# Expert 0's rows by products with a 0/1 mask instead of a gathered load, in a mixture of experts behind two transformer-like blocks

## The chip, the cores and the metric

The kernel runs on one core of one Trainium2 chip. It is a single launch that computes a network of about four layers for 512 tokens. The metric is the time of the whole launch on the device, in microseconds. The engines named here are TensorE (PE in the profile, PEld for its weight loads), VectorE (DVE), ScalarE (ACT), GpSimd (POOL) and SyncE (SP), which issues most DMA transfers. Each engine runs its own queue in order and waits on semaphores.

## The reference, cut to what matters

The change lies in the last layer, a mixture of 64 experts in 8 groups. Each of the 512 tokens picks a group, then two experts in it; an expert is a gated feed-forward net of width 512.

```python
def hier_moe(h, w_rg, w_re, w_gate, w_up, w_down):
    ...
    g_sel = jnp.argmax(g_logits, axis=-1)
    ...
    p_top, e_top = lax.top_k(jax.nn.softmax(e_logits, axis=-1), TOP_K)
    gate = p_group * p_top / jnp.sum(p_top, axis=-1, keepdims=True)
    expert_id = (g_sel[:, None] * EXPERTS_PER_GROUP + e_top).reshape(-1).astype(jnp.int32)
    ...
    xb = hf[tok_buf].reshape(n_blocks, MOE_BLOCK, D)

    def expert_block(args):
        xe, e = args
        return (jax.nn.silu(xe @ w_gate[e]) * (xe @ w_up[e])) @ w_down[e]

    yb = lax.map(expert_block, (xb, block_eid)).reshape(n_slots, D)
    y = jnp.zeros_like(hf).at[tok_buf].add(yb * gate_buf[:, None].astype(yb.dtype))
```

Everything is in float32. Before this layer stand a gated delta net, a retention layer, two convolutional feed-forward nets and a mixer of long convolutions and gated scans; the change leaves them alone.

## The kernel before, in words

The normalized tokens are kept as rows, `m.hn`, [128, 4, 1024]: token 128 t + p is on partition p. The same rows are written to `x_rows` in HBM. `Router.vector` finds for each token its group and its first and second expert, as 0/1 tables `wide[0]` and `wide[1]` over 64 experts, and their sum `wide[2]`. `Router.tensor` counts these: L4022 sums each expert's tokens, L4024 and L4026 give each token its order among those of an expert, in PSUM bank 0. VectorE makes slot numbers of it: every expert has 64 slots (`SLOTS`), slot 64 e + i holds the i-th token of expert e, and what exceeds 64 goes to overflow blocks behind the main loop. Eight products (L4031) of one 0/1 table of places and one table of blocks each turn "token to slot" into "slot to token", and VectorE writes the list as whole numbers: `x_of` (L4133) and `y_of` (L4134).

`Experts` runs the 64 experts in order. For expert e, GpSimd gathers 64 rows of `x_rows` by column e of `x_of` into `m.xe[e % 2]` (`gather_x`, L4155). TensorE turns them (`turn_x`, L4270, eight transposes into PSUM bank 0), VectorE copies them to `m.xeT` (`copy_x`, L4407), TensorE multiplies by the up and gate weights (`project`, L4282 and L4283, eight steps of two products with 512 columns), ScalarE and VectorE make the activation (L4392, L4420), TensorE turns it and multiplies by the down weights (L4293, L4299), ScalarE copies the result out (L4382) and GpSimd scatters it to `y_rows` (L4160). The order on TensorE is software pipelined by hand: `step` of expert e computes its projection, and ahead of the last of the eight steps (`ahead`) waits for the activation of expert e-1 and for the gathered rows of expert e+1 (`x_landed`).

SyncE loads the weights, 2.1 MB for each of the three matrices of an expert. Up and gate weights have two buffers, and expert 2 (`THIRD`) has a third pair of its own: `w_gate` in the tile hT and `w_up` in `m.hn`, which therefore must not be read any more. `load_up_apart` issues these two (L4218 after the transposes of the router, L4221 after the gathers of the first two experts have landed); all later loads stand behind them in SyncE's queue, each released by the projection or down product that frees its buffer (L4209).

`unread_products` (L310) are 128x128 products whose result nobody reads; 16 stand ahead of L4031 and 20 ahead of expert 0. The last two experts' outputs are combined in another way (`LATE`); their gate tables `m.late_gate` (L4439) and `m.late_diag` (L4426) are made by VectorE ahead of expert 0 and are first needed by `pause` behind expert 15.

Of the kernel before, what the change touches and what calls it, by code (L numbers as in the profile page):

```python
# [35 lines left out]
P = 128  # L36
# [44 lines left out]
LATE = 2  # L81
# [275 lines left out]
class Stream:  # L357
# [128 lines left out]
    def each(self, eng, chunks, per, body, splits=False):  # L486

        self.per = per
        for c in range(chunks):
            body(self.n + c, 0, c)  # L490
        self.skip(chunks, per, splits)
# [3491 lines left out]
class Router:  # L3983
# [3 lines left out]
    def __init__(self, k, m, norm):  # L3987
        self.k, self.m, self.norm = k, m, norm
        room = m.late
        self.logits = room.take(TT, N_GROUPS + NE)  # L3990
        self.small = room.take(8, TT, 8)
        self.one = room.take(16, TT)
        self.wide = room.take(4, TT * NE)
        self.rows = room.take(4, NE)
        self.at_place = room.take(2 * TT, P)
        self.at_block = room.take(2 * TT, NB)
        m.at_place, m.block_of = self.at_place, self.small[:, 7].rearrange("p t e -> p (t e)")[:, 0:2 * TT]
        m.late_spread = self.wide.rearrange("p n c -> p (n c)")[:, 0:LATE * T].rearrange("p (u t) -> p u t", u=LATE)
# [11 lines left out]
    def tensor(self, pe):  # L4010
# [16 lines left out]
        ins.then_inc(k.sem("router_counted"), 1)  # L4027
        k.unread_products(pe, 1, 16)
        for at in range(2 * TT):
            pe.wait_ge(k.sem("places_ready"), at + 1)  # L4030
            ins = pe.matmul(k.ps[:, 2, 0:NB], self.at_place[:, at, :], self.at_block[:, at, :], start=(at == 0), stop=(at == 2 * TT - 1))  # L4031
# [15 lines left out]
    def vector(self, dve, st):  # L4047
        k, m = self.k, self.m

        def do(ins):  # L4050
            st.done(ins)
            st.wait()
# [59 lines left out]
        place = self.wide[:, 2, :].rearrange("p (t e) -> p t e", t=TT)  # L4112
        dve.wait_ge(k.sem("router_counted"), 2)
        do(dve.scalar_tensor_tensor(place, order, float(SLOTS), each(base, NE), ALU.is_ge, ALU.mult))
        do(dve.scalar_tensor_tensor(place, place, float(SLOTS), order, ALU.mult, ALU.add))
# [17 lines left out]
        dve.scalar_tensor_tensor(m.x_of[:], k.ps[:, 2, 0:NB], float(NO_TOKEN), second_half, ALU.add, ALU.add).then_inc(k.sem("slots_ready"), 1)  # L4133
        dve.tensor_scalar(m.y_of[:], k.ps[:, 2, 0:NB], 2.0, m.half, ALU.mult, ALU.add).then_inc(k.sem("slots_ready"), 1)  # L4134

        found = self.small.rearrange("p a t e -> p (a t e)")[0:1, 0:OVER]
# [35 lines left out]
class Experts(Signals):  # L4172
# [6 lines left out]
    def __init__(self, k, m):  # L4179
        super().__init__(k, "moe", **{w: NE for w in ("x_turned", "x_copied", "act_turned")}, **{w: NE + 2 for w in ("up", "down", "silu", "acted")},  # L4180
                         act_copied=NE + 1, y_copied=NE + 1, gate_in0=8 * NE, x_in0=8 * NE, y_out0=8 * NE, y_free=NE + 1 - LATE)
        self.m = m
# [19 lines left out]
    def sync(self, sp):  # L4202
# [12 lines left out]
        def load_up_apart(e):  # L4215
            of = lambda src: k.ins[src][e:e + 1].rearrange("o (p k) n -> p (o k) n", p=P)
            sp.wait_ge(k.sem("hn_turned"), TT)
            sp.dma_start(m.w_gate[self.THIRD], of("w_gate_2")).then_inc(k.sem("apart_in"), 16)  # L4218
            for u in range(2):
                self.wait(sp, f"x_in{u}", 16)  # L4220
            sp.dma_start(m.w_up[self.THIRD], of("w_up_2")).then_inc(k.sem("apart_in"), 16)  # L4221
# [37 lines left out]
    def tensor(self, pe):  # L4259
# [13 lines left out]
        def x_landed(i, u):  # L4273
            self.wait(pe, f"x_in{u}", i * 16 + 16)

# [81 lines left out]

        k.unread_products(pe, 1, 20)
        x_landed(0, 0)
        turn_x(0)  # L4360
        self.steps(pe, step, early, behind, pause)
# [40 lines left out]
    def vector(self, dve):  # L4402
# [10 lines left out]
        def step(i, u, prev, next):  # L4413
            e = i * 2 + u
            if prev:
                copy_act(e, 1 - u)
            if next:
                copy_x(e + 1, 1 - u)
            self.wait(dve, "silu", e + 3)
            dve.tensor_tensor(m.act[u], m.silu[u], k.ps[0:SLOTS, 2 + u, :], ALU.mult).then_inc(self.sem("acted"), 1)  # L4420

        def spread_gates(t):
# [13 lines left out]

        for n in range(2):
            for t in range(TT):
                ins = dve.tensor_scalar(m.late_gate[:, n * TT + t, :], m.expert[:, NE - LATE:NE], m.block_of[:, n * TT + t:n * TT + t + 1], m.gates[:, n, t:t + 1], ALU.is_equal, ALU.mult)  # L4439
        ins.then_inc(k.sem("router_diff"), 1)  # L4440
        copy_x(0, 0)
        dve.wait_ge(k.sem("router_diff"), 3)
        spread_gates(0)
        self.steps(dve, step, lambda: copy_act(1, 0), lambda: copy_act(NE - LATE, 1), pause)
        copy_act(NE, 1)

    def gpsimd(self, pool):
# [3 lines left out]
        pool.wait_ge(k.sem("slots_ready"), 1)  # L4451
        for u in range(2):
            gather_x(k, m, pool, u, u).then_inc(self.sem(f"x_in{u}"), 16)
        self.wait(pool, "x_turned", 1)
        gather_x(k, m, pool, 2, 0).then_inc(self.sem("x_in0"), 16)
        pool.memset(m.no_rows, 0.0).then_inc(k.sem("router_zeros"), 1)
# [458 lines left out]
```

## Time and profile before

| | us |
|---|---|
| median of 3 runs | 3220.78 |
| lowest and highest run | 3219.91, 3223.1 |
| span of the profiled execution | 3221.5 |
| TensorE busy in it | 2990.5 |
| VectorE, ScalarE, GpSimd busy | 1141.7, 779.5, 901.7 |

The profile shows one execution. Of that execution the span is what the page gives as its own time. A busy TensorE is not one at its peak, since its records overlap; a float32 product is two records (16 products are 32). Times in the rows are us from the start of the span. "[idle before <-releaser]" is how long the engine had waited and what let it go. PEclk in a table of stretches is the clock that TensorE was granted as a share of 2.4 GHz; the DMA share is the mean busy share of 16 DMA engines and comes out at 1.01 when they are full.

### The profile page before, as it was taken

The page shows a single profiled execution, that of the slowest core. Times are in us where ns is not written, and L with a number is a line of the kernel's source. Part 1 is how long each engine was busy: PE and PEld are TensorE (multiplying, and loading weights), DVE is VectorE, ACT ScalarE, POOL GpSimd, SP SyncE. Part 2 cuts the span into 40 slices and gives each one's busy share as a digit, 9 for nine tenths or more (in the row PEclk, how much of TensorE's full clock was granted, in tenths as well). Part 3 has the DMA queues.
Part 4 walks back from the last instruction along what each step waited for, and adds up shares of the span by engine and source line. Part 5 has one row for each costly group of instructions (what it writes and reads, how often), then busy time and mean ns, then how long its engine had stood idle before and what let it go on. Part 6 is the DMA issues. An engine that isn't in the chain of part 4 may idle for free.

```text
span 3221.5 us, 39686 instructions
## 1 busy us (share of the span) xinstructions
PE 2990.5 (93%) x15996; PEld 1991.3 (62%) x15996; DVE 1141.7 (35%) x1865; ACT 779.5 (24%) x1104; POOL 901.7 (28%) x744
## 2 busy tenths in 40 slices
PE   7999999999999999999999999999888888888887
PEld 4778778878788667887879794455333333333332
DVE  4566585661620155224152774423111111111112
ACT  2435542232322333223143621111000000000001
POOL 2333534455354314445424230001111111111110
PEclk8999999999999999999999999999999999999999
DMA  7324454542222212223313021047999999999997
GB/s 259 89 82 132 132 183 170 195 131 78 85 92 93 78 40 79 92 96 107 86 60 92 29 89 51 1 169 269 408 411 422 414 406 413 406 410 403 406 397 291
DMA packets 256000, 631.61 MB, mean 196 GB/s; under 512 B 19217, under 2 KB 208690, under 8 KB 230525
## 3 DMA queue, kind: packets, MB, share of 16 engines
q1 hardware_dynamic: 245053, 619.23, 51.6%
q0 software_dynamic: 10240, 8.43, 0.8%
q8 instruction: 95, 1.56, 0.2%
q10 hardware_dynamic: 576, 2.10, 0.2%
q14 instruction: 36, 0.29, 0.0%
HBM read 633.88 MB, written 20.97 MB: 203 GB/s over the span
## 4 chain that ended last, share of the span: by engine, by line
PE 63%; DMA 20%; DVE 6%; issue 5%; PEld 3%; ACT 2%; POOL 2%; SPq 0%; PEldq 0%; DVEq 0%; POOLq 0%; ACTq 0%
DMA arena<-in_w_up 18%; PE ps L545 12%; PE ps L547 12%; PE ps L546 11%; PE ps L4282 9%; PE ps L3480 2%; POOL ring_parts L427 2%; PE ps L3698 2%; PE ps L4299 1%; PE ps L2520 1%; PE ps L2518 1%; PE ps L2519 1%; PEld ps L545 1%; PEld ps L547 1%; PEld ps L546 1%
## 5 line engine op out<-in xcount | busy, mean ns | idle before, releaser
L427 POOL TENSOR_TENSOR ring_parts<-ring,arena_parts 128x512 fp32r<-128x512 f32 x544 | 721.9, 1361 | 1007.7 <-ACT arena_parts L401 774.8
L545 PE MATMUL ps<-arena_parts,arena_parts 128*128 128x512 f32 (+1 forms) x2012 | 751.1, 373 | 9.4 <-DVE arena_parts L536 5.4
L547 PE MATMUL ps<-arena_parts,ring_parts 128*128 128x512 f32 (+1 forms) x2012 | 742.8, 369 | 0.0
L4282 PE MATMUL ps<-arena 128*64 128x512 f32 x1008 | 497.9, 652 | 142.6 <-DMA arena<-in_w_up 100.8
L546 PE MATMUL ps<-hT_parts,arena_parts 128*128 128x512 f32 (+1 forms) x1648 | 597.0, 362 | 0.0
L4283 PE MATMUL ps<-arena 128*64 128x512 f32 x1008 | 499.1, 653 | 0.0
L545 PEld LDWEIGHTS ps<-arena_parts,arena_parts 128*128 128x128 f32 x2012 | 379.7, 189 | 85.4 <-issue 7.6
L4282 PEld LDWEIGHTS ps<-arena 128*64 128x64 f32 x1008 | 145.6, 150 | 462.9 <-issue 461.0
L547 PEld LDWEIGHTS ps<-arena_parts,ring_parts 128*128 128x128 f32 x2012 | 379.8, 189 | 69.4
L401 ACT ACTIVATE arena_parts<-ring 128x2048 fp32r<-128x2048 f32 (+1 forms) x103 | 207.0, 2013 | 635.8 <-PE ps L547 596.3
L546 PEld LDWEIGHTS ps<-hT_parts,arena_parts 128*128 128x128 f32 x1648 | 310.3, 188 | 50.3 <-issue 0.2
L4411 DVE TENSOR_SCALAR arena<-ps 128x256 f32<-128x256 f32 x64 | 27.2, 425 | 786.9 <-PE ps L4293 786.9
L4160 POOL DMA_INDIRECT y_rows<-ring,y_of x62 | 61.9, 998 | 814.9 <-ACT ring L4382 798.3
L4299 PE MATMUL ps<-arena 128*64 128x512 f32 x1024 | 236.0, 603 | 9.3 <-DMA arena<-in_w_down 8.2
L546 PE MATMUL ps<-arena_parts,arena_parts 128*128 128x512 f32 x544 | 216.3, 398 | 0.0
L4392 ACT ACTIVATE arena<-ps 64x512 f32<-64x512 f32 x64 | 38.0, 595 | 638.9 <-PE ps L4283 638.9
L4299 PEld LDWEIGHTS ps<-arena 128*64 128x64 f32 x1024 | 68.6, 137 | 124.8 <-issue 112.4
L4283 PEld LDWEIGHTS ps<-arena 128*64 128x64 f32 x1008 | 145.3, 149 | 0.0
L546 PEld LDWEIGHTS ps<-arena_parts,arena_parts 128*128 128x128 f32 x544 | 103.4, 190 | 24.8 <-issue 1.0
L4382 ACT ACTIVATE ring<-ps 128x512 f32<-128x512 f32 x62 | 37.0, 597 | 288.7 <-PE ps L4299 288.7
L4155 POOL DMA_INDIRECT ring<-x_rows,x_of x64 | 62.5, 976 | 123.1 <-DVE y_of L4134 88.5
L2086 DVE SCALAR_TENSOR_TENSOR xT<-ps,mod,xT 128x512 f32<-128x512 f32 x28 | 21.0, 749 | 207.0 <-PE ps L547 206.9
(619 smaller groups left out, 3631.8 us busy)
## 6 DMA issues: line engine op xcount, KB each, us to landing
arena<-in_w_down SPq DMA_DIRECT2D x64, 2048.0 KB, 23.3
arena<-in_w_gate SPq DMA_DIRECT2D x62, 2048.0 KB, 17.9
arena<-in_w_up SPq DMA_DIRECT2D x62, 2048.0 KB, 22.4
ring<-in_ffn_up SPq DMA_DIRECT2D x44, 1024.0 KB, 5.1
arena<-in_ada_w SPq DMA_DIRECT2D x14, 2048.0 KB, 10.0
ring<-in_ret_w_in SPq DMA_DIRECT2D x24, 1024.0 KB, 5.2
ring<-in_ffn_down SPq DMA_DIRECT2D x16, 1408.0 KB, 7.0
ring<-in_gdn_w_in SPq DMA_DIRECT2D x16, 1024.0 KB, 5.7
```

Of the source, the lines that this page charges most:

```text
L401: act.activation(self.upper(room, n, kt, cols) if to is None else to, self.slot(n, kt, cols), ACT.Copy).then_inc(self.core.sem("chunk_roun ...
L427: ins = pool.tensor_tensor(lower[:, at], whole[:, at], upper[:, at], ALU.subtract)
L545: pe.matmul(out, upper[:, r], self.upper[r][:, part], start=(r == 0), stop=False)
L546: pe.matmul(out, upper[:, r], self.lower[r][:, part], start=False, stop=False)
L547: ins = pe.matmul(out, lower[:, r], self.upper[r][:, part], start=False, stop=(r == self.tiles - 1))
L3480: ins = pe.matmul(self.bank(j), w[:, r, j % 2 * P:(j % 2 + 1) * P], self.source(r), start=(first and r == rows[0]), stop=(last and r == ro ...
L3698: ins = pe.matmul(out(q), self.dft[:, q, t, at], of(q)[:, t, :], start=False, stop=(t == 1))
L4155: return pool.indirect_dma_start(m.xe[u], None, k.x_rows, at, bounds_check=T - 1, oob_is_err=False)
L4160: return pool.indirect_dma_start(k.y_rows, at, rows, None, bounds_check=2 * CHOICES - 1, oob_is_err=False)
L4282: pe.matmul(k.ps[upper, 2 + u, :], m.xeT[u][:, r, :], m.w_up[b][:, r, :], start=(r == 0), stop=(r == KD - 1))
L4283: ins = pe.matmul(k.ps[lower, 2 + u, :], m.xeT[u][:, r, :], m.w_gate[b][:, r, :], start=(r == 0), stop=(r == KD - 1))
L4299: ins = pe.matmul(k.ps[(upper, lower)[h], bank, :], m.actT[u][:, r, :], m.w_down[u][:, r, half], start=(r == 0), stop=(r == D_EXP // P - 1))
```

## The change

Expert 0's rows are no longer gathered. Behind the counts, VectorE makes `first_rows`, [128, 4, 64] in the region `wide[3]`: 1 where the order of a token in expert 0 is the slot's number and the token has chosen expert 0. TensorE multiplies: for each of the 8 groups of columns r (every eighth column of `m.hn`) and each of 4 token tiles, `m.hn[:, t, r::8]` as weights and `first_rows[:, t]` as 64 moving columns, summed over t. The result is what `turn_x` would have left, in PSUM bank 4, and VectorE copies it to `m.xeT[0]`. So the semaphores `moe_x_turned` and `moe_x_copied` get their first count in the router. GpSimd begins with the gathers of experts 1 and 2, both at once; expert 2's no longer waits for a turn. SyncE's load of expert 2's up weights waits for the new products too. The 16 unread products become 10 and the 20 become 4. The gate tables of the last two experts are made behind the activation of expert 2.

```diff
@@ Router.tensor
-        k.unread_products(pe, 1, 16)
+        k.unread_products(pe, 1, 10)
+        pe.wait_ge(k.sem("hn_copied"), TT)
+        pe.wait_ge(k.sem("places_ready"), 1)
+        for r in range(KD):
+            for t in range(TT):
+                ins = pe.matmul(k.ps[:, 4, r * SLOTS:(r + 1) * SLOTS], m.hn[:, t, r::KD], self.first_rows[:, t, :], start=(t == 0), stop=(t == TT - 1))
+        ins.then_inc(k.sem("moe_x_turned"), 1)
         for at in range(2 * TT):
-            pe.wait_ge(k.sem("places_ready"), at + 1)
+            pe.wait_ge(k.sem("places_ready"), at + 2)
@@ Router.vector
         dve.wait_ge(k.sem("router_counted"), 2)
+        do(dve.tensor_tensor(self.first_rows, m.place[:, 0:SLOTS].unsqueeze(1).to_broadcast([P, TT, SLOTS]), order[:, :, 0:1].to_broadcast([P, TT, SLOTS]), ALU.is_equal))
+        dve.tensor_tensor(self.first_rows, self.first_rows, place[:, :, 0:1].to_broadcast([P, TT, SLOTS]), ALU.mult).then_inc(k.sem("places_ready"), 1)
+        dve.wait_ge(k.sem("places_ready"), 1)
...
+        dve.wait_ge(k.sem("moe_x_turned"), 1)
+        dve.tensor_scalar(m.xeT[0].rearrange("p r s -> p (r s)"), k.ps[:, 4, :], 1.0, None, ALU.mult).then_inc(k.sem("moe_x_copied"), 1)
@@ Experts.sync, load_up_apart
+            self.wait(sp, "x_turned", 1)
             for u in range(2):
                 self.wait(sp, f"x_in{u}", 16)
@@ Experts.tensor
         def x_landed(i, u):
-            self.wait(pe, f"x_in{u}", i * 16 + 16)
+            self.wait(pe, f"x_in{u}", i * 16 + 16 * u)
...
-        k.unread_products(pe, 1, 20)
-        x_landed(0, 0)
-        turn_x(0)
+        k.unread_products(pe, 1, 4)
@@ Experts.vector: what stood ahead of the steps is now late_gates(), called behind step 2
+            if isinstance(e, int) and e == self.THIRD:
+                late_gates()
...
-        copy_x(0, 0)
@@ Experts.gpsimd
-        for u in range(2):
-            gather_x(k, m, pool, u, u).then_inc(self.sem(f"x_in{u}"), 16)
-        self.wait(pool, "x_turned", 1)
-        gather_x(k, m, pool, 2, 0).then_inc(self.sem("x_in0"), 16)
+        for e in range(1, 3):
+            gather_x(k, m, pool, e, e % 2).then_inc(self.sem(f"x_in{e % 2}"), 16)
```

TensorE between the router's counts and expert 0, before. `ring` holds the router's tables, `m.hn` and the gathered rows, `ident` is the unit matrix, `ps` is PSUM:

```order
L4026 MATMUL ps<-ring,ones 128x64
L310 MATMUL ps<-ident 128x128 x16
L4031 MATMUL ps<-ring 128x79 x8
L310 MATMUL ps<-ident 128x128 x20
L4270 MATMUL ps<-ident,ring 128x64 x8
L4282 MATMUL ps<-arena 64x512
```

The same place now:

```order
L4027 MATMUL ps<-ring,ones 128x64
L310 MATMUL ps<-ident 128x128 x10
L4034 MATMUL ps<-ring 128x64 x32
L4038 MATMUL ps<-ring 128x79 x8
L310 MATMUL ps<-ident 128x128 x4
L4296 MATMUL ps<-arena 64x512
```

The 32 new products stand ahead of the eight table products, 22 unread products are gone, and so are the eight transposes of expert 0's rows.

VectorE behind the list of slots, before (`x_of`, `y_of`, the overflow list, the gate sums, the late gate tables, the copy of expert 0's rows, the first diagonals):

```order
L4133 SCALAR_TENSOR_TENSOR x_of<-ps,ring 128x79
L4134 TENSOR_SCALAR y_of<-ps,arena 128x79
L4138 TENSOR_TENSOR ring<-ring,arena 1x960
...
L4147 TENSOR_TENSOR arena<-arena 128x4
L4439 TENSOR_SCALAR arena<-arena 128x2 x8
L4407 TENSOR_SCALAR arena<-ps 128x512
L4426 TENSOR_SCALAR par<-ident,arena 128x128 x4
```

The same place now:

```order
L4143 SCALAR_TENSOR_TENSOR x_of<-ps,ring 128x79
L4144 TENSOR_SCALAR y_of<-ps,arena 128x79
L4147 TENSOR_SCALAR arena<-ps 128x512
L4151 TENSOR_TENSOR ring<-ring,arena 1x960
...
L4432 TENSOR_TENSOR arena<-arena,ps 64x512
L4454 TENSOR_SCALAR arena<-arena 128x2 x8
L4440 TENSOR_SCALAR par<-ident,arena 128x128 x4
L4423 TENSOR_SCALAR arena<-ps 128x256
```

The copy of expert 0's rows (L4407 before, L4147 now) moved up right behind `y_of`, and the late gate tables moved down behind the third activation.

## Rows read from the trace of the kernel before

**Rows 1.** The page: the span, and the chain that ended last by line.
```profile
span 3221.5 us, 39686 instructions
...
DMA arena<-in_w_up 18%; PE ps L545 12%; PE ps L547 12%; PE ps L546 11%; PE ps L4282 9%; PE ps L3480 2%; POOL ring_parts L427 2%; PE ps L3698 2%; PE ps L4299 1%; PE ps L2520 1%; PE ps L2518 1%; PE ps L2519 1%; PEld ps L545 1%; PEld ps L547 1%; PEld ps L546 1%
```

**Rows 2.** Stretches: length, busy per engine, TensorE clock, DMA share, GB/s.
```profile
2200.00:2204.00 4.00, 4.00 (x29) 4.00 (x28) 3.59 (x16) 0.00 (x0) 1.80 (x2) 0.72 0.18 49
...
2212.00:2215.00 3.00, 2.97 (x18) 1.39 (x14) 0.00 (x0) 0.59 (x1) 0.00 (x0) 1.00 0.20 51
...
2241.00:2243.00 2.00, 2.00 (x12) 0.72 (x10) 0.00 (x0) 0.60 (x1) 0.00 (x0) 1.00 0.23 98
...
2249.00:2253.00 4.00, 4.00 (x24) 2.25 (x26) 1.70 (x3) 0.59 (x1) 0.00 (x0) 1.00 0.85 278
2253.00:2273.00 20.00, 20.00 (x100) 7.43 (x96) 1.70 (x3) 1.86 (x4) 3.94 (x4) 1.00 1.01 420
2273.00:3150.00 877.00, 736.00 (x3394) 302.38 (x3396) 103.81 (x188) 66.66 (x112) 111.28 (x114) 0.93 1.00 408
```

**Rows 3.** Timeline, router to expert 0: start, duration, engine, line, tiles, wait.
```profile
2189.46 3.79 PE L310 MATMUL ps<-ident 128*128 128x128 f32 x32
...
2190.68 0.42 DVE L4114 SCALAR_TENSOR_TENSOR ring<-ps,ring 128x256 f32<-128x256 f32 x1
2191.14 0.42 DVE L4115 SCALAR_TENSOR_TENSOR ring<-ring,ps 128x256 f32<-128x256 f32 x1
...
2194.57 3.43 PE L4031 MATMUL ps<-ring 128*128 128x79 f32 x16 [1.32 <-DVE ring L4128]
...
2197.19 0.32 DVE L4128 TENSOR_SCALAR ring<-arena 128x79 f32<-128x79 f32 x1
...
2198.48 0.29 DVE L4134 TENSOR_SCALAR y_of<-ps,arena 128x79 uint32<-128x79 f32 x1
...
2198.72 6.33 PE L310 MATMUL ps<-ident 128*128 128x128 f32 x40 [0.71 <-issue]
2199.54 1.32 POOL L4155 DMA_INDIRECT ring<-x_rows,x_of  x1 [88.55 <-DVE y_of L4134]
...
2201.16 0.95 POOL L4155 DMA_INDIRECT ring<-x_rows,x_of  x1 [0.31 <-issue]
...
2202.27 1.62 DVE L4439 TENSOR_SCALAR arena<-arena 128x2 f32<-128x2 f32 x8
2204.10 0.33 SPq L4221 DMA_DIRECT2D ring<-in_w_up  x1
...
2206.11 0.69 DVE L4407 TENSOR_SCALAR arena<-ps 128x512 f32<-128x512 f32 x1 [2.22 <-PE ps L4270]
...
2206.86 0.64 PE L4282 MATMUL ps<-arena 128*64 128x512 f32 x1 [0.78 <-DVE arena L4407]
...
2213.99 0.33 SPq L4209 DMA_DIRECT2D arena<-in_w_gate  x1
```

**Rows 4.** Timeline of TensorE: dense 64-column products, and unread ones at half clock.
```profile
1800.35 1.90 PE L3447 MATMUL ps<-arena 128*128 128x64 f32 x16
1802.09 1.73 PE L3451 MATMUL ps<-arena 128*128 128x64 f32 x14
...
2198.72 3.65 PE L310 MATMUL ps<-ident 128*128 128x128 f32 x16 [0.71 <-issue]
```

**Rows 5.** Timeline of VectorE: the first piece behind expert 2's activation.
```profile
2249.62 0.42 DVE L4411 TENSOR_SCALAR arena<-ps 128x256 f32<-128x256 f32 x1 [9.79 <-PE ps L4293]
```

**Rows 6.** Stretches with thin products, columns as in rows 2.
```profile
1800.50:1803.50 3.00, 3.00 (x30) 3.00 (x29) 2.79 (x9) 1.55 (x4) 0.00 (x0) 1.00 0.00 0
...
2195.00:2198.50 3.50, 3.01 (x15) 2.08 (x14) 2.93 (x15) 0.00 (x0) 0.00 (x0) 1.00 0.32 129
2199.00:2202.00 3.00, 3.00 (x16) 3.00 (x16) 2.79 (x9) 0.00 (x0) 2.16 (x2) 0.50 0.11 33
```

**Rows 7.** The line of the gathers: time from issue to landing, 64 of them.
```profile
DMA to landing us min/median/max: 2.9/9.8/11.2
```

More of the change, by code:

```diff
@@ L3994, in __init__ @@
         self.rows = room.take(4, NE)
+        self.first_rows = self.wide[:, 3, :].rearrange("p (t s) -> p t s", t=TT)
         self.at_place = room.take(2 * TT, P)
@@ L4180, in __init__ @@
         super().__init__(k, "moe", **{w: NE for w in ("x_turned", "x_copied", "act_turned")}, **{w: NE + 2 for w in ("up", "down", "silu", "acted")},
-                         act_copied=NE + 1, y_copied=NE + 1, gate_in0=8 * NE, x_in0=8 * NE, y_out0=8 * NE, y_free=NE + 1 - LATE)
+                         act_copied=NE + 1, y_copied=NE + 1, gate_in0=8 * NE, x_in0=8 * NE - 16, y_out0=8 * NE, y_free=NE + 1 - LATE)
         self.m = m
@@ L4435, in pause, with late_gates @@
                 spread_gates(t + 1)
[L4437 to L4440, printed above, removed]
-        copy_x(0, 0)
-        dve.wait_ge(k.sem("router_diff"), 3)
-        spread_gates(0)
+        def late_gates():
+            for n in range(2):
+                for t in range(TT):
+                    ins = dve.tensor_scalar(m.late_gate[:, n * TT + t, :], m.expert[:, NE - LATE:NE], m.block_of[:, n * TT + t:n * TT + t + 1], m.gates[:, n, t:t + 1], ALU.is_equal, ALU.mult)
+            ins.then_inc(k.sem("router_diff"), 1)
+            dve.wait_ge(k.sem("router_diff"), 3)
+            spread_gates(0)
         self.steps(dve, step, lambda: copy_act(1, 0), lambda: copy_act(NE - LATE, 1), pause)
```

## The prediction, as written before the result was known

> **What bounds the kernel now.** I read the page first, then the stage around the change in order of time, then the DMA share by stretch, and last the TensorE clock. The page gives a span of 3221.5 us and puts the largest single share of the chain that ended last, 18%, on loads of the experts' up weights [rows 1]. The windows say why: from 2273 to 3150 us the DMA engines are busy at a share of 1.00 and move 408 GB/s, while TensorE works 736 of 877 us [rows 2]. Those 877 us are a stream of weights, 6.3 MB for each expert, and no faster matmul shortens them. What can move is when that stream gets going. Its buffers come free one after the other as TensorE works through the first experts, so the start of expert 0 on TensorE sets it.
>
> In order of time [rows 3]: TensorE counts the choices and runs 16 unread products from 2189.46. VectorE meanwhile turns the counts into slot tables; the eight products that spread the tables out (L4031) start at 2194.57 and end at 2198.00, paced by VectorE. `x_of` follows (between L4031's end and 2198.77, the end of `y_of`), GpSimd gathers from 2199.54 and 2201.16, and both blocks of rows are in by 2204.10, when SyncE, which waited for both, issues expert 2's up weights. TensorE fills the time with 20 unread products until 2205.05, turns expert 0's rows, VectorE copies them (2206.11, 0.69 us), and expert 0's first product starts at **2206.86**. It ends at about 2213.95, where SyncE is let go.
>
> **The change part by part.** I follow the two engines that meet at expert 0.
>
> VectorE gets two operations of 128x256 ahead of L4114. L4114 and L4115 are of that size, 0.42 us each and 0.46 from start to start [rows 3], so the new mask is ready at 2191.56 and everything behind it, the slot tables too, is 0.92 us later: the last table at 2197.51 + 0.92 = 2198.43.
>
> TensorE: ten unread products instead of 16. The 16 are 32 records in 3.79 us, 0.118 each, so 20 records end at 2191.83, after the mask. Then 32 products with 64 columns and full 128x128 weights, two records each: 64 records. The trace has such records at 1800 us, 16 of them from 1800.35 until the next line starts at 1802.09, 0.109 each [rows 4]. 64 x 0.109 = 6.98, so they end at 2198.81. The eight table products queue behind them, by then with all their inputs there: 16 records at 0.114 (between the 0.109 of 64 columns and the 0.118 of 128) and a tail of 0.15 make 1.97: they end at 2200.78 instead of 2198.00, **2.78 later**. This is the price of the change, and the work that hides most of the 6.98 is the wait for VectorE that stood there before.
>
> Behind that, on VectorE: `x_of` and `y_of` end 2.78 later, at 2201.55, and now the copy of expert 0's rows comes next, 0.69 [rows 3]: 2202.24. On TensorE: the end of the stage cost 0.72 (2198.00 to 2198.72), then four unread products, 8 x 0.118 = 0.94: 2200.78 + 0.72 + 0.94 = **2202.44**. The later of the two counts. Expert 0 starts at 2202.4 instead of 2206.86: **4.4 us earlier**. What goes is the chain of gather, 16 unread products, turn and copy; what is late next is TensorE's own queue.
>
> The overflow list and the gate sums now come behind the copy on VectorE. They are about 3.5 us (2198.77 to 2202.27, [rows 3]), so they end near 2205.8, and VectorE is next wanted when expert 1's rows are turned, after expert 0's products, which now end at 2209.5. The late gate tables (1.62 us at 2202.27, and four 128x128 diagonals behind them) go behind expert 2's activation. VectorE idles 9.79 us there before its next piece [rows 5], so I cost them at nothing; without that cover they would cost their 1.62 us and the diagonals.
>
> GpSimd: one gather fewer, and expert 2's rows are asked for at once, not after a turn. The first gather now starts at 2199.54 + 2.78 = 2202.3, the second is in at 2204.10 + 2.78 = 2206.9. TensorE asks for expert 1's rows ahead of the last of the eight steps of expert 0, 7/8 of 7.1 us after its start: 2208.6. That holds with 1.7 us to spare. Nothing more of the gathers is on the path.
>
> SyncE waits for the products too and, as before, for both gathers. Expert 2's up weights go out at 2206.9, not 2204.1, and all later loads stand behind that instruction in the queue. The next, for expert 3, is wanted when expert 0's products end, now 2209.5, so the queue itself holds nobody up. But counted from expert 0's start the 2.1 MB go out 7.2 us later, into a stage that has more to carry. At 420 GB/s, the rate at a full share of 1.01 [rows 2], they need 5.0 us. The free DMA time that they find there is (1.01 - 0.20) x 3 = 2.4 in 2212:2215, 0.78 x 2 = 1.6 in 2241:2243 and 0.16 x 4 = 0.6 in 2249:2253: 4.6 us. So **0.4 us** of the 4.4 are given back. The bounds are 0 (small gaps between those holes) and 2.6 (only the first hole can be used).
>
> From 2253 on nothing refers to an absolute time: the weights stream, TensorE's and VectorE's turns and the scatters are released by one another, so the end moves with the start. **Sum: 4.4 - 0.4 = 4.0 us.** The profiled span of 3221.5 becomes 3217.5. It lies 0.7 above the median of the three runs, 3220.78, inside their 3219.91 to 3223.1; against the median the forecast is **3216.8 us**.
>
> **The clock.** The granted clock was 1.00 (2.4 GHz) through 3 us of 64-column records, but it was 0.50 (1.2 GHz) in 2199:2202, after a stretch in which TensorE was busy 3.01 of 3.50 us with 79-column products that waited for VectorE [rows 6]. So an engine that shows as busy can still lose its clock here, and the new stretch of 88 records (64 + 16 + 8) is thin too, if without gaps. At the low clock 16 records took 3.65 us where 16 took 1.90 at the high one [rows 4]. The Trainium skill ("TensorE: Matmul & The Clock Gate", Part 1) describes the half clock as the state of an idle engine, which activity releases. By that rule alone the gapless stretch stays at 2.4 GHz and the result is the 3216.8 above; the fall at 2199 speaks against reading it that simply, since no comparable idle time stood before it.
>
> **Rivals.**
> *A dip.* The clock falls once between 2195 and 2210 and comes back. The one in the trace holds 0.50 through all of 2199:2202 [rows 6], so it costs half of 3 us or a little more, say 1.7: gain 4.0 - 1.7 = 2.3, 3218.5. For it: the same stretch of the program had such a dip. Against: the gaps that stood there are filled now.
> *The low clock stays: slower.* The clock falls half way through the new products and is back only inside expert 0. A record then takes 3.65 / 16 = 0.23 us instead of 0.11 or 0.12 [rows 4]: 32 of the 64 cost 0.12 more each (3.8), the 16 table records 1.8, the last 8 unread ones 0.9, and expert 0 begins at half clock (1.7 again): 8.2 in all. Then 3216.8 + 8.2 = 3225.0, slower than before by 4.2. It turns to a loss once the low clock has taken back 4.0 us, which is when the 88 records take 0.16 us on average instead of 0.11. For it: the dip at 2199 came out of thin products. Against it: the clock of 1.00 in 1800.5:1803.5, though wider products stood on both sides there.
> *Weights late.* Only the first DMA hole can be used: 2.6 of the gain go, 4.4 - 2.6 = 1.8, 3219.0. For it: the holes at 2241 and 2249 are short, and each ends when TensorE lets a buffer go.
> *The gather is missed after all.* A gather lands in 9.8 us at the median and 2.9 at best [rows 7]. With 9.8 the rows of expert 1 come at 2212.1 instead of before 2208.6, and TensorE waits 3.5: gain 0.5, 3220.3, and the change does not do what it says. Against: 9.8 is the number of the saturated stage; in 2200:2204 the DMA share was 0.18 [rows 2].
>
> **How the numbers follow.** Forecast 0.50, dip 0.17, weights late 0.13, low clock 0.08, gather 0.04, and 0.08 for a weight stream that falls in step differently and takes several us more or less. The range takes in all of these but the low clock and most of the last, and above and below them the 1 us by which the median of three runs can sit beside the true one: 3215.0 to 3221.5. 0.2% is 6.4 us, about what a measurement of this kernel can tell from no change; every named case lies inside it, so faster gets 0.07 and slower 0.05 (a longer low clock, or the stream out of step), and same 0.88.
>
> **What would show it.** Right: expert 0's first product at about 2202.4, 4.4 us earlier, with 64 records of the new products in 7.0 us; no unread product ends later than VectorE's copy by over 0.3; expert 2's up weights issued near 2206.9; the DMA holes before 2215 and at 2241 mostly gone. Wrong: a clock of 0.50 inside the new products or in expert 0; a wait of TensorE for gathered rows ahead of expert 0's last step; a first wait for expert 3's or 4's weights, which there was not before; a span that moves though expert 0's start does not.

## The result, and the profile after

The changed kernel takes 3230.2 us at the median of 9 runs (3227.23 to 3233.22), the kernel before 3222.5 beside it (9 runs, 3219.91 to 3223.1). The ratio is 1.0028, 95% interval 1.002 to 1.0036: 0.28% slower. The median lies 13.4 us above the forecast of 3216.8 and 8.7 above the upper end of its range, 3221.5. The profiled execution has a span of 3231.3 us, 9.8 more than before. It is one of the longer executions of the nine (3233.08 us on the device), so it shows more of a loss than the 7.7 us between the medians.

TensorE of the changed kernel from the last of the router's counts (L4027) to expert 0 (L4296), and expert 0's down products (L4313). Columns: start, duration from the first start to the last end, engine, line, operation, shapes, how many, and the idle time before:

```profile
2188.98 0.88 PE L4027 MATMUL ps<-ring,ones 128*128 128x192 f32 x6
2189.70 2.45 PE L310 MATMUL ps<-ident 128*128 128x128 f32 x20
2191.98 15.41 PE L4034 MATMUL ps<-ring 128*128 128x64 f32 x64
2207.19 3.64 PE L4038 MATMUL ps<-ring 128*128 128x79 f32 x16
2211.54 2.04 PE L310 MATMUL ps<-ident 128*128 128x128 f32 x8 [0.71 <-issue]
2213.52 1.12 PE L4296 MATMUL ps<-arena 128*64 128x512 f32 x1
...
2225.53 5.35 PE L4313 MATMUL ps<-arena 128*64 128x512 f32 x16 [0.56 <-issue]
```

Against [rows 3]: the new products (L4034) start where the working put them, 2191.98 against 2191.83, and then take 15.4 us for 64 records instead of 7.0, which is 0.24 each. Expert 0 starts at 2213.52 instead of 2206.86. All of this trace is 0.23 us late (VectorE's last operation ahead of the counts stands at 2187.07 and at 2186.84 before), so the change itself makes 6.4 us of it. VectorE is not what is slow: its last table ends at 2198.66, 0.23 off the working, and then it waits.

```profile
2198.34 0.32 DVE L4138 TENSOR_SCALAR ring<-arena 128x79 f32<-128x79 f32 x1
2210.87 0.24 DVE L4142 TENSOR_SCALAR ring<-ps 128x79 f32<-128x79 f32 x1 [12.21 <-PE ps L4038]
2211.51 0.68 DVE L4147 TENSOR_SCALAR arena<-ps 128x512 f32<-128x512 f32 x1
```

What the new products are made of, by their line in the changed kernel (duration in ns: lowest, median, highest; first and last start; shapes). The new thing stands in the first row, the weight load:

```profile
L4034 PEld LDWEIGHTS ps<-ring x64: 313/335/336, 2191.9 to 2206.9; 128*128 128x128 f32 x64
L4034 PE MATMUL ps<-ring x64: 385/442/450, 2192.0 to 2207.0; 128*128 128x64 f32 x64
```

A load of 128x128 float32 weights takes 0.335 us here. The 16 records at 1800 us from which the prediction took its 0.109 [rows 4] are of L3447, whose loads have a mean of 192 ns. The same 64 records in stretches of time, with busy us (and records started) of TensorE and of its loads, the granted clock, DMA share and GB/s:

```profile
2192.00:2195.00 3.00, 3.00 (x13) 3.00 (x14) 1.00 0.88 317
2196.00:2206.00 10.00, 10.00 (x43) 10.00 (x44) 0.50 0.05 20
```

13 records in 3 us and 43 in 10 us are 0.23 a record at either level of the clock. The pace does not follow the clock here, so it is the loads that make the new products twice as long; the experiments below test it. But the clock fell too, from 2.4 to 1.2 GHz, while TensorE was busy without a gap, and it stayed there until 2216. Behind the new products that costs time; there is another, shorter one at 2226.5 (columns as above, with VectorE, ScalarE and GpSimd between PEld and the clock):

```profile
2200.00:2204.00 4.00, 4.00 (x19) 4.00 (x18) 0.00 (x0) 0.00 (x0) 0.00 (x0) 0.50 0.02 4
2214.00:2216.00 2.00, 2.00 (x6) 0.47 (x4) 1.40 (x8) 0.00 (x0) 1.69 (x3) 0.50 0.12 31
2216.50:2218.00 1.50, 1.50 (x10) 0.56 (x8) 0.00 (x0) 0.00 (x0) 1.02 (x1) 1.00 0.06 22
2226.50:2229.50 3.00, 3.00 (x10) 1.14 (x8) 0.00 (x0) 0.00 (x0) 0.00 (x0) 0.50 0.97 400
```

SyncE of the changed kernel, expert 2's up weights (L4235) and the loads that queue behind them (L4222):

```profile
2217.43 0.33 SPq L4235 DMA_DIRECT2D ring<-in_w_up  x1
2221.92 0.33 SPq L4222 DMA_DIRECT2D arena<-in_w_gate  x1
2230.91 0.33 SPq L4222 DMA_DIRECT2D arena<-in_w_down  x1
```

Expert 3's gate weights go out at 2221.92, 7.9 us after the 2213.99 of [rows 3]: the 6.7 of expert 0's start and 1.3 for the half clock in its first products. The down weights go out at 2230.91, 9.6 us after the 2221.28 of before; expert 0's 16 down products took 5.35 us, most of them at half clock, 1.7 more than the 3.65 that they took before at full clock. The two rows of before:

```profile
2217.59 3.65 PE L4299 MATMUL ps<-arena 128*64 128x512 f32 x16 [0.56 <-issue]
2221.28 0.33 SPq L4209 DMA_DIRECT2D arena<-in_w_down  x1
```

The span is 9.8 longer. From there on the two traces run alike: from 2290 to 3170 both have a DMA share of 1.00 and 409 GB/s.

The sum against the forecast, then, in this execution: new products +8.4, table records +1.7 (3.64 instead of 1.97), unread ones +1.1 (2.04 instead of 0.94), expert 0 at half clock +1.3, its down products +1.7. That is 14.2 us late against a start of expert 0 forecast 4.4 us early, and 14.2 - 4.4 = 9.8 is the difference of the spans. That it agrees to the tenth is chance: the sum leaves out the 0.4 us that the forecast gave back, and each term is read to 0.1 or 0.2. The last term belongs to this execution only; in a second profile of the changed kernel (after_again, below) the down products took 3.65.

### The profile page after: what moved, and what is told of

Same layout as the page of the kernel before. It is cut to its first block, busy times and chain, and to the rows that moved or that the text cites. A ratio compares the mean times of both kernels' runs of the same rounds, so it can differ in the third digit from the quotient of the medians.

```text
span 3231.3 us, 39711 instructions
## 1 busy us (share of the span) xinstructions
PE 3004.1 (93%) x16008; PEld 2002.5 (62%) x16008; DVE 1142.2 (35%) x1867; ACT 779.2 (24%) x1104; POOL 900.9 (28%) x743
## 4 chain that ended last, share of the span: by engine, by line
PE 63%; DMA 20%; DVE 5%; issue 5%; PEld 3%; ACT 2%; POOL 2%; SPq 0%; PEldq 0%; DVEq 0%; POOLq 0%; ACTq 0%
DMA arena<-in_w_up 18%; PE ps L545 12%; PE ps L547 11%; PE ps L546 11%; PE ps L4296 9%; PE ps L3480 2%; POOL ring_parts L427 2%; PE ps L3698 2%; PE ps L4313 1%; PE ps L2520 1%; PE ps L2519 1%; PE ps L2518 1%; PEld ps L545 1%; PEld ps L547 1%; PEld ps L546 1%
## 5 line engine op out<-in xcount | busy, mean ns | idle before, releaser
L4296 PE MATMUL ps<-arena 128*64 128x512 f32 x1008 | 500.7, 655 | 142.9 <-DMA arena<-in_w_up 96.8
L4296 PEld LDWEIGHTS ps<-arena 128*64 128x64 f32 x1008 | 146.2, 150 | 465.3 <-issue 464.4
L4313 PE MATMUL ps<-arena 128*64 128x512 f32 x1024 | 238.2, 608 | 6.3 <-DMA arena<-in_w_down 5.2
L4313 PEld LDWEIGHTS ps<-arena 128*64 128x64 f32 x1024 | 69.3, 138 | 123.3 <-issue 113.9
```

The lines of the kernel that those rows point to most:

```text
L4296: pe.matmul(k.ps[upper, 2 + u, :], m.xeT[u][:, r, :], m.w_up[b][:, r, :], start=(r == 0), stop=(r == KD - 1))
L4313: ins = pe.matmul(k.ps[(upper, lower)[h], bank, :], m.actT[u][:, r, :], m.w_down[u][:, r, half], start=(r == 0), stop=(r == D_EXP // P - 1))
```

## The experiments

Theory: the new products are slow since their weights, `m.hn[:, t, r::8]`, are read with a step of 8 elements along a row, and the load pays for that. Rival: the low clock made them slow. The kernel before ran beside every batch; its medians there were between 3221.89 and 3222.16 us.

### The load by itself: e2_probe

The kernel before, with eight groups of eight unread products on the tile xT instead of the 20 ahead of expert 0, and 16 plain ones between the groups. The step of the weights (1, 2, 4, 8, 16 elements), the partitions and the operand vary.

```diff
-        k.unread_products(pe, 1, 20)
+        some = k.ident[:, 0:SLOTS]
+        for n in range(8):
+            pe.matmul(k.ps[:, 1, 0:SLOTS], flat[:, 0:P], some, start=True, stop=True)
...
+        for n in range(8):
+            pe.matmul(k.ps[:, 1, 0:SLOTS], flat[:, 0:8 * P:8], some, start=True, stop=True)
...
```

> The kernel before, with the 20 unread products ahead of expert 0 replaced by eight groups of eight unread products on the tile xT, 16 plain unread products between the groups to hold the clock. All products are float32, so 16 records a group, and have 64 moving columns: weights of 128 columns that lie side by side; every 2nd, 4th, 8th and 16th column; every 8th on 64 partitions only; eight transposes of every 8th column on 128 partitions (8 records); plain weights with every 8th column as the moving operand. Theory S (the step between the weights' columns costs, whatever the clock): 0.11 us a record for side by side, about 0.24 for every 8th, with weight loads of 0.19 and 0.335; 0.11 for the moving operand with the step. Theory N (64 columns or the chain of products itself is slow, the step does not matter): every group alike. For 64 partitions S expects 0.11 if the number of partitions decides, as the transposes of gathered rows in the trace suggest (0.12), and 0.24 if the step alone does; the transposes on 128 partitions tell whether it is the form of the product. The time of the kernel is longer by the added records and says nothing.

One run, 3275.32 us, since the probe is long. Its weight loads, in the order: side by side, every 2nd, 4th, 8th, 16th element, and every 8th on 64 partitions:

```profile
L4362 PEld LDWEIGHTS ps<-ident,xT x16: 192/192/192, 2202.2 to 2203.9; 128*128 128x128 f32 x16
L4365 PEld LDWEIGHTS ps<-ident,xT x16: 196/196/197, 2207.6 to 2209.4; 128*128 128x128 f32 x16
L4368 PEld LDWEIGHTS ps<-ident,xT x16: 310/330/330, 2213.1 to 2216.5; 128*128 128x128 f32 x16
L4371 PEld LDWEIGHTS ps<-ident,xT x16: 315/335/336, 2222.0 to 2225.5; 128*128 128x128 f32 x16
L4374 PEld LDWEIGHTS ps<-ident,xT x16: 294/312/312, 2229.4 to 2232.6; 128*128 128x128 f32 x16
L4377 PEld LDWEIGHTS ps<-ident,xT x16: 309/332/333, 2236.6 to 2240.2; 64*128 64x128 f32 x16
```

and two of its groups on the time line:

```profile
2202.36 1.90 PE L4362 MATMUL ps<-ident,xT 128*128 128x64 f32 x16
2222.11 3.91 PE L4371 MATMUL ps<-ident,xT 128*128 128x64 f32 x16
```

The clock was 1.00 in all eight groups; behind two of them, the one of step 4 and the one on 64 partitions, it was 0.50 for 3.4 us in the plain products. With step 1 the 16 records take 1.90 us, the number of [rows 4]; with step 8 they take 3.91, 0.24 each, the number of the changed kernel, and the load has the same 335 ns. A step of 2 costs next to nothing (1.99 us for the 16), one of 4 already costs nearly all (3.84), and on 64 partitions a step of 8 costs as much as on 128 (332 ns, 4.01 us), so the step decides and not the number of partitions. A step of 8 in the moving operand costs little: 2.04 us, with loads of 198 ns. The theory holds without the kernel around it. I also read a transpose with strided weights (186 ns) as unaffected, because it is no slower than a plain load of a product. That reading was wrong; e5_sorted_before shows why.

### The changed kernel with weights side by side: e1_straight

```diff
-                ins = pe.matmul(k.ps[:, 4, r * SLOTS:(r + 1) * SLOTS], m.hn[:, t, r::KD], ...
+                ins = pe.matmul(k.ps[:, 4, r * SLOTS:(r + 1) * SLOTS], m.hn[:, t, r * P:(r + 1) * P], ...
```

> The changed kernel with the weights of the 32 new products taken from 128 columns side by side instead of every eighth. Expert 0 then works on its rows with their columns in another order, so its output is not the reference's; the amount of work is the same. Theory S (the step costs): the 64 records take 7.0 us instead of 15.4, the clock holds or dips once, expert 0 starts near 2202.5 to 2205, and the kernel takes 3 to 4 us less than the kernel before if the clock holds, ratio 0.9988 to 0.9991, and 0.9993 to 0.9998 with a dip. Theory N (64-column products are slow or lose the clock whatever their weights): the records stay at 0.24 us and the ratio stays at 1.002 to 1.003. Theory C (the low clock is what costs, and thin products lose it): 0.11 at first, 0.22 from about 2196 on, ratio 1.0005 to 1.0015.

3218.37 us (10 runs, 3216.88 to 3222.91), ratio 0.999, interval 0.998 to 0.9999. Its TensorE:

```profile
2193.32 7.26 PE L4034 MATMUL ps<-ring 128*128 128x64 f32 x64
2200.41 1.96 PE L4038 MATMUL ps<-ring 128*128 128x79 f32 x16
```

The kernel leaves out the right order of columns for expert 0 and nothing of the work. One slice of one operand takes away the whole loss, about 11 us. The 64 records take 7.26 us (7.1 to the start of L4038; the prediction had 6.98), the table records 1.96 (1.97). They start 1.5 us late, since this execution had the low clock in the unread products ahead of them. With it falls the rival that the stage is slow whatever the weights. It does not part the loads from the low clock, since both are gone here; e6_wide does that.

### A right kernel with the weights side by side: e4_sorted and e4b_again

The columns of `m.hn` and of `x_rows` are stored sorted by r, so that group r is 128 columns side by side; the experts' transposes read them so as well, and the overflow blocks load their up and gate weights with rows in the matching order.

```diff
-            act.activation(m.hn[:, t, :].rearrange("p (b c) -> p b c", b=2), k.ps[...], ...
+            act.activation(m.hn[:, t, :].rearrange("p (r b q) -> p r b q", r=KD, b=2), k.ps[...].rearrange("p b (q r) -> p r b q", r=KD), ...
-                ins = pe.transpose(..., m.xe[u][:, r::KD], ...)
+                ins = pe.transpose(..., m.xe[u][:, r * P:(r + 1) * P], ...)
```

> The changed kernel with the rows of the tokens stored in another column order (all columns p*8+r of one r side by side, written so by ScalarE's four copies), so that the weights of the new products and of the 64 experts' transposes lie side by side; the result is the reference's. Theory S: new products 7.0 us, and the kernel is 3 to 4 us shorter than before if the clock holds (ratio 0.9988 to 0.9991). Theory N: as the changed kernel, 1.002 to 1.003. ScalarE's four copies, 1.11 us each, have a step of eight on their PSUM side now; if that costs, they take 1.5 to 2 us each and the gathers come later by up to 2 us, which has 1.7 us of room.

> e4_sorted once more, beside e7_filled on the same chip: ratio 0.9987 again and a start of expert 0 at 2202.4. A ratio of 1.000 would say that its gain was one of chance, one below 0.998 that more is won than the start of expert 0 shows.

3218.5 us (10 runs), ratio 0.9987, interval 0.9978 to 0.9997; in another batch 3218.03 (11 runs), 0.9987, interval 0.9978 to 0.9996. It is the fastest kernel here whose result is the reference's, 0.13% faster than before, and it does what the prediction said of the change. TensorE, SyncE and GpSimd of e4_sorted:

```profile
2191.55 7.29 PE L4034 MATMUL ps<-ring 128*128 128x64 f32 x64
2198.68 1.96 PE L4038 MATMUL ps<-ring 128*128 128x79 f32 x16
2201.35 1.13 PE L310 MATMUL ps<-ident 128*128 128x128 f32 x8 [0.71 <-issue]
2202.41 0.64 PE L4296 MATMUL ps<-arena 128*64 128x512 f32 x1
2209.43 0.71 PE L4284 MATMUL ps<-ident,ring 64*128 64x64 f32 x8
...
2202.17 1.92 POOL L4168 DMA_INDIRECT ring<-x_rows,x_of  x1 [91.39 <-DVE y_of L4144]
...
2207.22 0.33 SPq L4235 DMA_DIRECT2D ring<-in_w_up  x1
```

Expert 0 starts at 2202.41, forecast 2202.44; the gather at 2202.17, forecast 2202.3; expert 2's up weights at 2207.22, forecast 2206.9; and the turn of expert 1's rows (L4284) follows at 2209.43 with no wait. In the profile of e4b_again expert 0 starts later, at 2204.67: there the clock was 0.50 from 2189.1 to 2192.5, ahead of the new products.

### The order of columns alone: e5_sorted_before

> The kernel before with nothing but the other order of columns of e4_sorted: rows sorted by r, the experts' transposes read 128 columns side by side. It tells apart whether e4_sorted gains by the order itself or by the new products. Theory (a column step costs only in loads of float32 weights, not in transposes, whose strided loads took 0.186 us in e2_probe): nothing changes, ratio 1.000, expert 0 starts at 2206.9. Rival (the strided transposes of all experts cost too): ratio 0.998 or lower, as e4_sorted had, and a mean record of L4270 shorter than before.

The kernel before with e4_sorted's order of columns: 3222.44 us (10 runs), ratio 1.0002, interval 0.9993 to 1.0011. So e4_sorted gains by the new products, not by the order. But the means of a load by line say something that I had expected of the rival only. First the kernel before, then e5_sorted_before (the columns at the end: busy us and mean ns | idle):

```profile
L4270 PEld LDWEIGHTS ps<-ident,ring 64*128 64x128 f32 x512 | 62.6, 202 | 2.6 <-issue 2.4
L4315 PEld LDWEIGHTS ps<-ident,xT 128*128 128x128 f32 x32 | 3.6, 141 | 0.0
```

```profile
L4270 PEld LDWEIGHTS ps<-ident,ring 64*128 64x128 f32 x512 | 38.2, 141 | 2.6 <-issue 2.4
```

A transpose's load takes 141 ns with columns side by side and 202 with a step of 8. Strided transposes do pay, eight of them 1.09 us instead of 0.71. That the time stays fits a stream in which TensorE is busy 736 of 877 us [rows 2]. The first fence is of the kernel **before**: the cost of a column step stood in its trace, in L4270 beside L4315.

### Loads or clock: e6_wide, after_again, e9_first_load_only

Strided weights as in the changed kernel, but 128 moving columns instead of 64: the mask is passed twice and VectorE's copy takes the first half of each result alone.

```diff
-                ins = pe.matmul(k.ps[:, 4, r * SLOTS:...], m.hn[:, t, r::KD], self.first_rows[:, t, :], ...
+                ins = pe.matmul(k.ps[:, 4 + r // 4, r % 4 * P:...], m.hn[:, t, r::KD], self.first_rows[:, t, :].unsqueeze(1).to_broadcast([P, 2, SLOTS]), ...
```

> The changed kernel with the weights of the new products strided as they are, but with 128 moving columns (the mask twice, the second half is not read) instead of 64. It tells the two parts of the loss apart: the slow loads and the clock. A record stays at 0.24 us if the load sets it (15.4 us for the 64), and TensorE has twice the columns in that time. Theory A (the clock fell since the strided products carry few columns in their time): the clock holds at 1.00 through them, the table records take 1.97 instead of 3.64, the four unread ones 0.94 instead of 2.0, expert 0 begins at full clock: start about 2210.7, 3 us earlier than in the changed kernel, time about 3227. Rival B (the slow loads themselves bring the low clock): clock 0.50 as in the changed kernel, start at 2213.5, time 3230. Rival C (the record is set by columns too and grows to 0.4 us or more at half clock): later than 2215.

> The kernel with 128 moving columns (e6_wide) once more, for its clock: 0.50 nowhere in the new products and the table records, as in its first profile, says that the wider products hold the clock; a low stretch of over 10 us there says that its first profile was one of chance.

> The changed kernel once more, for its clock: its first profile showed 0.50 from 2195.6 to 2216, the other kernels show low stretches of 3.5 to 4 us whose place differs from profile to profile. Theory: the new products are 0.24 us each again (15.3 us, their loads 0.335), and a low stretch of more than 10 us over their end, the table records and the start of expert 0 comes again. Rival: the long low stretch was one of chance; here it is 4 us or lies elsewhere, and expert 0 starts 2 to 3 us earlier than in the first profile.

e6_wide took 3226.25 us (10 runs), ratio 1.0017, interval 1.0007 to 1.0026; e9_first_load_only is the same kernel and took 3227.44 (8 runs), 1.0016, interval 1.0006 to 1.0027. The changed kernel once more: 3229.66 (8 runs), 1.0023, interval 1.0013 to 1.0033. TensorE of e9_first_load_only, then of after_again:

```profile
2207.79 1.91 PE L4038 MATMUL ps<-ring 128*128 128x79 f32 x16
2210.41 1.13 PE L310 MATMUL ps<-ident 128*128 128x128 f32 x8 [0.71 <-issue]
```

```profile
2208.88 3.65 PE L4038 MATMUL ps<-ring 128*128 128x79 f32 x16
2213.33 2.05 PE L310 MATMUL ps<-ident 128*128 128x128 f32 x8 [0.80 <-issue]
```

The load rows of L4034, first of e6_wide, then of after_again, and the clock of e6_wide over its new products:

```profile
L4034 PEld LDWEIGHTS ps<-ring x64: 315/335/336, 2189.3 to 2204.3; 128*128 128x128 f32 x64
```

```profile
L4034 PEld LDWEIGHTS ps<-ring x64: 315/335/338, 2193.6 to 2208.6; 128*128 128x128 f32 x64
```

```profile
2190.00:2200.00 10.00, 10.00 (x44) 10.00 (x44) 4.32 (x22) 0.00 (x0) 0.00 (x0) 1.00 0.21 85
```

The new products take their 15 us in both, so the load sets them and not the columns or the clock. The low clock behind them is a second cost: with 64 columns it came in both profiles (2195.6 to 2216, and 2199 to 2220) and made the table records 3.65 instead of 1.91; with 128 columns the clock was 1.00 through new products and table records, in both profiles. By the medians the clock is worth 2 to 4 us (3229.66 and 3230.2 against 3227.44 and 3226.25), though the intervals of the ratios overlap. By the rows it is 2.7 us up to expert 0 (1.7 in the table records, 0.9 in the unread ones), and 1.3 and 2.2 in expert 0's first products.

The mean granted clock of each run tells why the medians show less than the rows: the long low stretch seems not to come every time. Of the 17 runs of the changed kernel 12 have a mean of 0.968 to 0.971, the two profiled ones among them, and a median of 3231.6 us. The other five have 0.972 to 0.974 and a median of 3227.35, the time of e6_wide. All 18 runs of e6_wide and its repetition have 0.972 or more. So the low clock costs some 4 us where it comes. (None of the five was profiled, so this rests on their mean clocks alone.) The rest, some 5 us against before, is the loads: more than half of the loss of 7.7, and e1_straight says that without the slow loads there is no loss.

The time is what theory A expected, 3227. The start of expert 0 is not: counted as in the table below it comes 1.0 us earlier than in the first profile of the changed kernel and 2.7 earlier than in the second, instead of 3. Both profiles with 128 columns and the second of the changed kernel have a short low stretch just ahead of the new products, which the first has not. Why the clock falls with 64 columns and not with 128 is not shown.

### Does the start set the end: e3_delay

```diff
-        k.unread_products(pe, 1, 20)
+        k.unread_products(pe, 1, 60)
```

> The kernel before with 60 unread products ahead of expert 0 instead of 20: 80 more records of 0.118 us, so expert 0 starts 9.4 us later, 8 if the half clock that stands there before now falls into a part with more records. If the end moves with the start of expert 0, as the prediction took it, the kernel is longer by 8 to 10 us, ratio 1.0025 to 1.003. If the stream of weights hides part of a later start, the ratio is below 1.0015. The gathers and expert 2's up weights are not delayed here, so the difference between this slope and 1 is what the DMA side can take up.

3232.43 us (7 runs), ratio 1.0031, interval 1.002 to 1.0043. Expert 0 starts 8.9 us later, counted from VectorE's last operation ahead of the counts, and the kernel takes about 10 us more. In the profiled execution, counted from the start of the span, expert 0 comes 6.6 us later (2213.45) and the span is 7.3 longer (3228.8). Nothing behind expert 0 takes the delay up. The same count for all kernels:

| | that operation to expert 0, us | against before | median against the before of its batch |
|---|---|---|---|
| before | 20.0 | | |
| e3_delay | 29.0 | +8.9 | +10.5 |
| changed kernel | 26.5 | +6.4 | +7.7 |
| changed kernel again | 28.2 | +8.1 | +7.8 |
| e6_wide, and again | 25.5, 25.5 | +5.5 | +4.1, +5.6 |
| e5_sorted_before | 19.7 | -0.4 | +0.3 |
| e1_straight | 17.5 | -2.5 | -3.6 |
| e4_sorted, and again | 15.8, 17.4 | -4.3, -2.7 | -3.5, -4.1 |

The first numbers are from one execution each, the last are medians; they go together within 2 us.

### The late gate tables alone: e8_late_alone

> The kernel before with one part of the change alone: the last experts' gate tables are made behind expert 2's activation. Theory: it lies in VectorE's idle time on both sides, 1.000 within the interval, and expert 0 starts where it did. Rival (the tables hold up the turn of expert 3's rows, or their absence ahead of expert 0 lets something earlier): 0.9995 or less, or 1.001 or more.

3222.01 us (10 runs), ratio 1.0, interval 0.999 to 1.0009, and expert 0 starts 20.1 us after that operation. The interval leaves room for 3 us either way. The rows say more: behind the tables VectorE still idles 7.35 us before its next piece (9.79 before, [rows 5]), so they cost nothing there.

```profile
2241.11 0.88 DVE L4428 TENSOR_SCALAR par<-ident,arena 128x128 f32<-128x128 f32 x4
2249.33 0.42 DVE L4411 TENSOR_SCALAR arena<-ps 128x256 f32<-128x256 f32 x1 [7.35 <-PE ps L4293]
```

### Filling a wait: e7_filled

```diff
+            k.unread_products(pe, 1, 5)
```

(ahead of the wait for the activation, in the kernel e4_sorted).

> e4_sorted with five unread 128x128 products put ahead of the wait for expert 0's activation, the place where the clock fell to 0.50 during expert 0's down products (5.35 us for 16 records, 3.65 before). Theory (the dip follows from TensorE's wait for the activation, and comes there since none stood earlier): with the wait filled the 16 down records take 3.65 and everything behind is 1.7 us earlier, time 3216.8. Rival 1 (the fall is due anyway, and moves to the next thin place): the dip shows up later, no gain or 1 us. Rival 2 (the unread products themselves delay the activation's transposes): 0.5 to 1 us slower than e4_sorted.

3219.91 us (11 runs), ratio 0.9993, interval 0.9984 to 1.0002. e4b_again, in the same batch, had 0.9987. No gain; the intervals overlap, so no certain loss either. The theory behind it rested on a single profile. TensorE of e7_filled, then of e4b_again, at expert 0's down products:

```profile
2214.41 3.65 PE L4313 MATMUL ps<-arena 128*64 128x512 f32 x16 [0.56 <-issue]
```

```profile
2215.03 3.65 PE L4313 MATMUL ps<-arena 128*64 128x512 f32 x16 [0.56 <-issue]
```

The stretch that was to be filled away was not there in e4b_again either. That execution of the same kernel as e4_sorted had its low clock at 2189.1 to 2192.5, mostly in the unread products ahead of L4034, and not at 2213 to 2216.5. Whether filling the wait helps in those executions that have it is left open.

## Why the prediction was wrong, point by point

*The step that failed* is the term for the new products: "The trace has such records at 1800 us ... 0.109 each [rows 4]. 64 x 0.109 = 6.98". They were not such records. Shape, columns and type agreed, the layout of the weights did not: side by side there, every eighth float here. They measured 15.4 us. With the quick loads (7.1 us) e4_sorted starts expert 0 where the forecast had it, within 0.3 us in its first profile; in its second, with a low stretch ahead of the new products, it starts 2.2 us later. The mechanism of the gain was right, and this term alone was off by more than the gain.

What could have been seen: the diff says `r::KD` in plain sight, and the kernel before has transposes with the same step, L4270, at 202 ns a load beside 141 for L4315. From that 1.43 the term would have come to some 10 us, not 15, but it would have been a bound: 3 us more on a gain of 4, and with the first rival's dip of 1.7 no gain at all.

The Trainium skill ("TensorE: Matmul & The Clock Gate", section "LDWEIGHTS (loading the stationary operand)") makes the time of a load a matter of the number of columns. For float32 the runs here disagree: 128 columns took 192 ns side by side and 335 with a step of 8.

*The clock.* The rival was named ("the clock falls half way through the new products and is back only inside expert 0") and it is what both profiles of the changed kernel show, with 0.08 as its chance; judged by the mean clock of each run it came in 12 of 17. Its terms came out for the table records (+1.8 priced, +1.7 measured), the unread ones (+0.9, +1.1) and expert 0 (1.7 priced, 1.3 and 2.2 measured). Its main term, 3.8 for 32 records at half clock, did not: 0.23 a record is what the slow loads take at full clock too, so the fall cost nothing inside L4034. That rival alone gave 3225.0. With the loads' 8.4 in place of its 3.8, and the 1.7, 1.1 and 1.3 as measured, 3216.8 becomes 3229.3, beside a median of 3230.2. With quick loads it did not come true: in e1_straight and in three profiles of e4_sorted and its variant the clock was 1.00 through the new products. The rule that the Trainium skill states ("TensorE: Matmul & The Clock Gate", Part 1), half clock for an idle engine, does not cover the fall at 2195.6: TensorE and its loads had no gap from the start of the new products, 2191.98, up to it.

*Right:* VectorE's 0.92 and the start of the new products (2191.98 against 2191.83); the table records at 1.97; the copy never the later of the two; the gathers in time, in e4_sorted with none waited for; the late gate tables at nothing (by the rows of e8_late_alone); the end moving with expert 0's start (e3_delay). The 0.4 us that the later up weights give back is too small for these runs to show, and the larger bound of 2.6 is not supported: e4_sorted gains 3.5 to 4.1 us at the median where its two starts are 4.3 and 2.7 us earlier.

*The range* ended at 3221.5 because every unknown in it was a matter of waits. The one operation that was new to the kernel was entered as known.

## What to carry to other kernels

When a duration is borrowed from another line, compare the access pattern as well as shape and type, the weights' step above all: a float32 product with every eighth element as weights took 0.24 us a record, and 0.11 with the same elements side by side (e4_sorted). Here it is cured at no cost that these runs can tell (1.0002 in e5_sorted_before, ScalarE's four copies at 1.11 us as before) where the tile is written, not where it is read. And a new operation on the path gets its own bounds, however familiar it looks.

## What the runs showed of the hardware

- Loads of 128x128 float32 weights: 192 ns with step 1, 196 with 2, 330 with 4, 335 with 8, 312 with 16, and 332 with 8 on 64 partitions. Loads of transposes: 141 side by side, 202 on 64 partitions and 186 on 128 with a step of 8. The moving operand with a step of 8: 198.
- The granted clock fell to 0.50 within 64-column products whose loads take 335 ns, with TensorE busy all the time, in both profiles of the changed kernel, and stayed there for some 20 us, into expert 0. It did not with 128 columns at the same loads and the same 0.24 us a record, in two profiles. The mean granted clock of the runs agrees: 0.971 or less in 12 of 17 runs with 64 columns, in none of 18 with 128.
- A low stretch of about 3.4 us is found in every profile between 2180 and 2230, in some two or three, and one of 6.8 us in e8_late_alone (2213.3 to 2220.1). Its place changes between executions of one kernel (2213 in e4_sorted, 2189 in e4b_again). A cost or gain that rests on the place of such a stretch in one profile is worth a second profile first.
